# Sums of the up projection's weights, and four low parts of its row sums, moved from VectorE to GpSimd

## The reference, cut to what matters

```python
def conv_ffn(h, w_up, conv_w, conv_b, w_down):
    T = h.shape[1]
    u = h @ w_up                                  # (1024 x 1024) @ (1024 x 5632)
    up = jnp.pad(u, ((0, 0), (CONV_W - 1, 0), (0, 0)))
    c = conv_b + sum(up[:, j:j + T] * conv_w[j] for j in range(CONV_W))
    gate, val = jnp.split(c, 2, axis=-1)
    return (jax.nn.gelu(gate) * val) @ w_down
```

## Time and profile before, and how to read it

| | |
|---|---|
| median of 3 runs | 3161.99 us (3160.99 to 3164.35) |
| the profiled execution's own time | 3159.94 us |
| its span in the trace | 3158.2 us |
| PE busy | 3071.4 us, 97% |
| DVE busy | 1975.9 us, 63% |
| ACT busy | 1629.8 us, 52% |
| POOL busy | 198.8 us, 6% |
| mean granted clock of PE | 0.994 of full speed |

### The profile page before, as it was taken

The page is one execution under the profiler, slowest core; times in us unless marked ns, Lnnn a source line. Parts: engine busy times, 40 slices in busy tenths (PEclk is TensorE's granted clock), DMA queues, the critical chain, the costliest instruction groups (busy, mean ns, idle before and its releaser), DMA issues. The chain is left out here.

```text
span 3158.2 us, 45373 instructions
## 1 busy us (share of the span) xinstructions
PE 3071.4 (97%) x18052; PEld 2559.1 (81%) x18052; DVE 1975.9 (63%) x3114; ACT 1629.8 (52%) x2713; POOL 198.8 (6%) x373
## 2 busy tenths in 40 slices
PE   7999999999999999999999999998998999999998
PEld 5988889898888888888788778886686888878886
DVE  7544444544444578752589463447859888878865
ACT  6343443524433347513698444415736777764455
POOL 2000000000000000000344100000000000000000
PEclk9999999999999999999999999999999999999999
DMA  6102111010334467412310541110062222245664
GB/s 219 52 24 76 42 57 61 27 61 31 128 118 149 139 214 250 147 41 73 94 36 3 149 132 54 29 57 27 15 219 68 84 90 81 81 148 188 234 231 152
DMA packets 204931, 322.19 MB, mean 102 GB/s; under 512 B 29340, under 2 KB 117249, under 8 KB 204721
## 3 DMA queue, kind: packets, MB, share of 16 engines
q1 hardware_dynamic: 182800, 241.37, 23.8%
q0 software_dynamic: 20848, 77.85, 7.1%
q10 hardware_dynamic: 1072, 0.07, 0.0%
HBM read 271.97 MB, written 47.28 MB: 101 GB/s over the span
## 5 line engine op out<-in xcount | busy, mean ns | idle before, releaser
L401 DVE TENSOR_TENSOR W_rounded<-W,W_rounded 128x2048 fp32r<-128x2048 f32 (+2 forms) x119 | 202.2, 1699 | 275.8 <-ACT W_rounded L392 272.1
L392 ACT ACTIVATE W_rounded<-W 128x2048 fp32r<-128x2048 f32 (+1 forms) x107 | 168.3, 1573 | 213.3 <-DMA W<-in_ab_w_in 60.7
L5120 PE MATMUL G<-down_ring_rounded 128*128 128x512 f32 x924 | 213.1, 392 | 4.2 <-DVE down_ring_rounded L5183 4.2
L1171 PE MATMUL G<-W_rounded,HT_rounded 128*128 128x512 f32 x640 | 212.0, 412 | 0.0
L2420 PE MATMUL G<-HT_rounded,W_rounded 128*128 128x512 f32 (+1 forms) x768 | 207.9, 356 | 1.6 <-DVE qk_conv L1429 1.6
L1215 PE MATMUL G<-HT_rounded,W_rounded 128*128 128x512 f32 (+1 forms) x768 | 206.7, 355 | 1.0 <-PEq L666 1.0
L5120 PEld LDWEIGHTS G<-down_ring_rounded 128*128 128x128 f32 x924 | 174.0, 189 | 41.2 <-DVE down_ring_rounded L5183 5.1
L3666 PE MATMUL G<-W_rounded,HT_rounded 128*128 128x512 f32 x640 | 200.1, 394 | 0.0
L2420 PEld LDWEIGHTS G<-HT_rounded,W_rounded 128*128 128x128 f32 x768 | 137.0, 189 | 25.5 <-issue 5.3
L1215 PEld LDWEIGHTS G<-HT_rounded,W_rounded 128*128 128x128 f32 x768 | 136.3, 189 | 21.4 <-issue 1.2
L1406 DVE SCALAR_TENSOR_TENSOR c_state<-c_state,decay_all,CC 128x514 f32<-128x514 f32 x64 | 48.0, 750 | 154.6 <-PE CC L1200 154.6
(11 more groups left out here) (647 smaller groups left out, 7906.4 us busy)
## 6 DMA issues: line engine op xcount, KB each, us to landing
up_w_in<-in_w_up SPq DMA_DIRECT2D x44, 512.0 KB, 3.9
W<-in_ab_w_in SPq DMA_DIRECT2D x20, 1024.0 KB, 8.7
W<-in_w_mod SPq DMA_DIRECT2D x8, 2048.0 KB, 8.2
x_rows<-r_xt POOLq DMA_DIRECT2D x32, 512.0 KB, 5.6
down_ring<-act_rows SPq DMA_DIRECT2D x25, 512.0 KB, 4.2
W<-in_c_w_out SPq DMA_DIRECT2D x24, 512.0 KB, 7.1
r_xt<-x_rows POOLq DMA_DIRECT2D x24, 512.0 KB, 4.7
W<-in_w_in SPq DMA_DIRECT2D x12, 1024.0 KB, 5.1
```

Source lines behind the costliest of these rows:

```text
L392: ins = a.activation(self.half(key, True)[:, at], self.half(key, False, False)[:, at], ACT.Copy)
L401: ins = v.tensor_tensor(self.half(key, False)[:, at], self.half(key, False, False)[:, at], self.half(key, True)[:, at].bitcast(F32), ALU.s ...
L1171: ins = pe.matmul(G[:, K.par(key), :], x[y][:, 4 * kh + k, r * P:(r + 1) * P], wv[z][:, k, :], start=(kh == 0 and k == 0 and (y, z) == SPL ...
L5120: ins = pe.matmul(G[:, bank[r], :], x[y][:, m, r * P:(r + 1) * P], w[z][:, m, :], start=(p in (P1, P5) and q == 0 and m == 0 and (y, z) == ...
```

## The change

All four sums of every column tile are made by POOL, as are the last four low parts of the row sums (t3 and t4, both halves). For tile 0 this stands in POOL's row queue ahead of the store of row block 6; for tile 1 and the low parts, in the opening of the up part, ahead of the semaphore clearing; for the tiles from 2 on, behind it. The low parts count on the sums' semaphore, so counts from tile 2 on are higher by four. The operations, their shapes and their order within a tile are the same, as is the order of what DVE keeps.

```diff
-    def queue(self, g, source, later=False):
+    def queue(self, g, source, later=False, between=None):
...
         for r in range(self.n):
+            if between is not None:
+                between(g, r)
             if r < self.n_store:
                 self.store_x(g, r)
...
     def first_lo(v, s):
         if s == 11:
             up_gate_lo(K, v, 0)
-            up_sums(K, v, 0)
             rows.value(v, 5)
...
+    def first_sums(g, r):
+        if r == XT - 2:
+            g.wait_ge(*K.freed_by[("out2", 2, 1)])
+            up_sums(K, g, 0)
...
-        sp.wait_ge(K.s_sum, 4 * old + 4)
+        sp.wait_ge(*up_summed(K, old, 4))
...
+def up_summed(K, j, n):
+
+    return K.s_sum, 4 * j + n + (4 if j >= 2 else 0)
+
+
+def up_sums(K, g, j):
+
+    up_landed(K, g, j, 0)
+    up_landed(K, g, j, 1)
     if j >= 2:
-        v.wait_ge(K.s_p[7], j - 1)
+        g.wait_ge(K.s_p[7], j - 1)
...
+    g.tensor_tensor(s12[:, 0, :], a21, a22, ALU.add).then_inc(K.s_sum, 1)
+    g.tensor_tensor(s43[:, 1, :], a11, a21, ALU.subtract).then_inc(K.s_sum, 1)
+    g.wait_ge(*up_summed(K, j, 1))
+    g.tensor_tensor(s12[:, 1, :], s12[:, 0, :], a11, ALU.subtract).then_inc(K.s_sum, 1)
+    g.wait_ge(*up_summed(K, j, 3))
+    g.tensor_tensor(s43[:, 0, :], a12, s12[:, 1, :], ALU.subtract).then_inc(K.s_sum, 1)
...
     def gpsimd(g):
         rows.left(g)
+        up_sums(K, g, 1)
+        for n, half in LOWS[6:10]:
+            g.wait_ge(s_xh, TERMS.index((n, half)) + 1)
+            g.tensor_tensor(part_of(n, half, 0), exact[n](half), part_of(n, half, 1).bitcast(F32), ALU.subtract)\
+                .then_inc(K.s_sum, 1)
         for s in K.spent:
             ins = g.sem_clear(s)
         ins.then_inc(s_ready, 1)
         rows.stored(g)
+        for j in range(2, NJ):
+            up_sums(K, g, j)
...
         def term_ready(n):
-            pe.wait_ge(s_xl, LOWS.index((n, 1)) + 1)
+            at = LOWS.index((n, 1)) + 1
+            if at > 6:
+                pe.wait_ge(K.s_sum, 8 + at - 6)
+            else:
+                pe.wait_ge(s_xl, at)
...
         up_sum_lo(K, v, 0, 1)
-        up_sums(K, v, 1)
-        for n, half in LOWS[6:8]:
-            term_lo(n, half)
         c11(0)
         up_last_lo(K, v, 1)
         c12(0)
         up_sum_lo(K, v, 1, 0)
-        for n, half in LOWS[8:10]:
-            term_lo(n, half)
         for j in range(1, NJ):
...
             gelu_arg(j - 1)
-            if j + 1 < NJ:
-                up_sums(K, v, j + 1)
-            else:
+            if j == NJ - 1:
                 K.down_lo(v, 0)
             gated(j - 1)
```

More of the change, by code:

```diff
@@ L2765, in gpsimd @@
             prev.left(g)
-        B.queue(g, source, prev is not None and tail is not None)
+        B.queue(g, source, prev is not None and tail is not None, None if tail is None else tail[3])
     def tensor(pe):
@@ L4330, in out2_part @@
                      parts=split_at, n_parts=4, ahead=0, presplit=[("out2", 0, 0), ("out2", 0, 1)],
-                     prev=diff, tail=(load_first, first_hi, first_lo))
+                     prev=diff, tail=(load_first, first_hi, first_lo, first_sums))
     K.up_rows_done = rows.finished
@@ L4404, in up_landed @@
     eng.wait_ge(K.up_in[n % 3], 16 * (n // 3 + 1))
-def up_sums(K, v, j):
-    up_landed(K, v, j, 0)
-    up_landed(K, v, j, 1)
+def up_summed(K, j, n):
[3 more added lines that the diff above has]
+    up_landed(K, g, j, 1)
     if j >= 2:
-        v.wait_ge(K.s_p[7], j - 1)
+        g.wait_ge(K.s_p[7], j - 1)
     s12, s43 = K.up_sum[0][0][j % 2][0], K.up_sum[1][0][j % 2][0]
     a11, a12, a21, a22 = up_w(K, j, 0, 0), up_w(K, j, 0, 1), up_w(K, j, 1, 0), up_w(K, j, 1, 1)
[L4415 to L4420, removed]
+    g.tensor_tensor(s12[:, 0, :], a21, a22, ALU.add).then_inc(K.s_sum, 1)
[4 more added lines that the diff above has]
+    g.tensor_tensor(s43[:, 0, :], a12, s12[:, 1, :], ALU.subtract).then_inc(K.s_sum, 1)
 def up_gate_hi(K, a, j):
@@ L4450, in up_sum_hi @@
 def up_sum_hi(K, a, j, w):
-    a.wait_ge(K.s_sum, 4 * j + (4 if w else 3))
+    a.wait_ge(*up_summed(K, j, 4 if w else 3))
     if j >= 2:
@@ L4459, in up_sum_lo @@
     v.wait_ge(K.s_hs[w], j + 1)
-    v.wait_ge(K.s_sum, 4 * j + 4)
+    v.wait_ge(*up_summed(K, j, 4))
     s, h = K.up_sum[w]
@@ L4901, in room @@
             sp.wait_ge(K.s_la, NJ)
-            sp.wait_ge(K.s_sum, 4 * NJ)
+            sp.wait_ge(*up_summed(K, NJ - 1, 4))
         if s == 1:
```

## The result

The changed kernel takes 3221.32 us (median of 4 runs, 3219.83 to 3225.79) beside 3163.17 us for the kernel before in the same comparison: ratio 1.0187 [1.0175, 1.0199], 58 us slower. The profiled run took 3220.12 us, 3218.3 of them span. The direction is the forecast's, and the time is still inside the range; the loss is twice the 29.4 us of the sum.

A forecast was written before the change was run, and what follows sets the result against it. PE was taken to bound the up part, with gains only in the opening. Losses of 25 us in later tiles and 4.4 us in the opening, 29.4 us, gave 3191 us for the median; range 3154 to 3225 us.

The forecast's parts named there:

- the 29.4 us of the sum: Whole kernel: forecast loss, 25 us in the later tiles plus 4.4 us in the opening.
- The bound: Up part: PE full behind the opening, 11.6 us idle in it; DVE and ACT's round has 0.5 us slack per tile.
- The mechanism: Where POOL's operation meets a DVE operation with two SBUF inputs, one stands while the other reads; 1.2 us per sum.
- The price of one operation: POOL's sums and low parts: 1.3 us for 128x512, 2.5 us for 128x1024; reading 512 values of two inputs holds 1.2 us.
- the number of holds in a tile: Later tiles: 0.6 us behind c22 plus one gap of 1.2 us, 1.8 us before slack.
- one of the two: Gaps where POOL can come in, before the convolution's second step and before gelu_arg; one counted, at 1.2 us.
- the fourth falls in the sigmoid's pause: Later tiles: POOL's fourth sum was taken to run while DVE waits for ACT's sigmoid before gated, with no hold counted.
- 0.6 + 1.2 - 0.5 = 1.3: Each later tile: hold behind c22, plus one gap, less slack, in us lost; 25 us over 19 tiles.
- -5.2 and +9.6: Opening: 5.2 us won from PE's waits, 9.6 us lost as half of POOL's 19 us of reading holds DVE.
- no blocking: First rival, whole kernel: POOL reads in short bursts, so no blocking that matters; 3156.8 us, chance 0.22.
- DVE keeps its turn: Second rival: POOL stands until DVE's pause, a tile loses 0.1 us at most, opening breaks even; 3163 us, chance 0.18.
- The third with both gaps: Rival of longer holds: POOL takes both gaps, 2.5 us per tile; 3214 us, chance 0.15 including its 1.6 us reading case.

The follow-up runs named there:

- the copies: Changed kernel, but from tile 2 on POOL copies one block of weights into each of the four places instead of summing two; 3177.33 us against 3162.43, ratio 1.0043.
- the fills: Changed kernel, but from tile 2 on POOL fills the four places with a constant and reads nothing; 3167.23 us, ratio 1.0013.
- the run of the opening alone: Changed kernel, but sums from tile 2 on back on DVE behind gelu_arg; 3166.42 us against 3163.28 for the kernel before, ratio 1.0011.

## Why the prediction was right in direction and half the size

- **The bound** was read rightly: PE full in the loop, nothing to win there, and a slack of DVE and ACT's round of 0.5 us; three kernels measure it at 0.39 to 0.43 us.
- **The mechanism** was right: one engine stands while the other reads. In the loop it is shown from both sides, by moving the reads into the pause (the loop's loss goes) and by taking the reads away at the old moment (it goes as well).
- **The price of one operation** was right: 1.28 us for 512 values, taken as 1.3; 2.40 us for 1024, taken as 2.5. A full hold is 0.9 to 1.1 us, taken as 1.2.
- **What failed is the number of holds in a tile.** "No row shows POOL waiting at such a gap, so I count one of the two", and "the fourth falls in the sigmoid's pause". The runs show that in the loop POOL gets in between DVE's operations that read two SBUF inputs, wait or no wait: `sum_lo` and `gelu_arg` are held, back to back, by 1.10 and 1.07 us. And a POOL operation that stands takes 2.25 us itself, so the four last 8.5 us instead of 5.2; the fourth starts at 2643.07, not in the pause that begins at 2646.29. Nor does the first sum always start with `c22`: it starts 0.5 or 6 us ahead of it (2636.76, 2655.80), and in the second case it meets operations that the count left out. All four hold DVE: (6.55 / 2) = 3.3 us a tile, less 0.43, is 2.8, where 0.6 + 1.2 - 0.5 = 1.3 was forecast. Over 20 tiles that is 56 us; 25 were forecast, for 19 tiles.
- **The rows that misled** are the pair at 1580.07, where POOL stood behind two of DVE's operations and held neither. I read a priority into it. It is not that those POOL operations read little (128 values of one input): in the opening a whole sum stood behind three of DVE's operations and held none (2382.45). What decides who goes first stays open.
- **The rule of the Trainium skill** (SBUF — State Buffer, section Who interferes with whom), that the second to start stands for the whole of the first, was put aside for that row. In the loop the sums agree with it within some 0.1 us: the operation of L4457 at 2655.89 meets a sum of which 1.19 us are left and is held by 1.06. So do the copies within 0.2 us (held by 0.37 of 0.52 us left and 0.30 of 0.51), the adds that read PSUM (L4830: 675 to 692 ns, also beside POOL) and the fills. The opening's row does not: DVE's operation at 2383.42 started 1 us after POOL's, and POOL stood.
- **The opening**: -5.2 and +9.6, net +4.4, against +2.4 in the trace and +3 us in the run of the opening alone. The sign is right. Of the 2.5 us to be won at the scaled rows, PE's wait there shows 1.8 (2.8 to 1.0 us); with tile 0's sums alone, holds on the operations ahead of these rows took back 2.1.
- **The rivals**: no blocking (3156.8 us) and DVE keeps its turn (3163 us) are refuted in the loop by DVE's own durations, though in the opening DVE does keep its turn at 2382.45. The third with both gaps, 3214 us, came nearest; it named the right step and had the lowest chance.

## What to carry to other kernels

When work moves to GpSimd, list the VectorE operations that read two SBUF inputs while it runs (here the scaling with one was held too): where they meet, one of the two stands, so two streams that overlap run largely one after the other. Which one stands could not be read off beforehand here. Ask whether VectorE's round has a pause for it and make GpSimd wait for the start of that pause; here one wait was worth 55 us. Work that sits in a pause already wins nothing by leaving it.

## What was not expected of the hardware

- **The turns are strict in the loop, and not always in the opening.** In the loop the engines alternate even between operations without any gap, and the recorded duration of both doubles: POOL's 1.28 to 2.27, DVE's 1.22 to 2.32 us. In the opening one sum of POOL stood through three operations of DVE in a row and took 4.45 us. A view of mean durations alone would call both slow.
- **A free engine's time is not the measure.** With the same POOL operations in the pause each is 1.29 us and the loop costs nothing, though POOL was busy only 36% of the stretch (123.56 of 340 us) in the slow version.
- **The operation of DVE with one tensor input, the scaling at L597, is held too**: 1.77 for 0.75 us beside POOL's sums.
